# A convolution feed-forward on one core: seven products of quarters on every other weight step

## What is computed

```python
def conv_gated_ffn(h, w_up, conv_w, conv_b, w_down):
    u = h @ w_up                                   # 512 x 1024 times 1024 x 5632
    up = jnp.pad(u, ((0, 0), (1, 1), (0, 0)))
    u = up[:, :-2] * conv_w[0] + up[:, 1:-1] * conv_w[1] + up[:, 2:] * conv_w[2] + conv_b
    gate, val = u[..., :D_FF], u[..., D_FF:]
    return (jax.nn.silu(gate) * val) @ w_down      # D_FF = 2816
```

## Time and profile before

| | us |
|---|---|
| time, median of 3 runs (lowest, highest) | 3782.29 (3782.15, 3783.75) |
| the profiled execution, its own time | 3782.21 |
| its span, first to last instruction | 3780.4 |
| PE busy | 3712.6 (98%) |
| PEld busy | 3116.3 (82%) |
| DVE busy | 2598.0 (69%) |
| ACT busy | 1591.2 (42%) |
| POOL busy | 53.9 (1%) |
| granted TensorE clock, mean | 0.995 |

### The profile page before, as it was taken

How to read it: one execution, slowest core, us unless ns; L and a number is a source line. 1 busy time by engine, 2 the same in 40 slices (tenths; PEclk the granted TensorE clock), 3 DMA queues, 4 the chain that set the end, 5 groups by cost and what they waited for, 6 DMA issues and landing times. The chain is left out here.

```text
span 3780.4 us, 52721 instructions
## 1 busy us (share of the span) xinstructions
PE 3712.6 (98%) x20462; PEld 3116.3 (82%) x20462; DVE 2598.0 (69%) x3639; ACT 1591.2 (42%) x2347; POOL 53.9 (1%) x52
## 2 busy tenths in 40 slices
PE   9999999999999999999999999999999999999998
PEld 7998864988998998786598899865888888888887
DVE  8875666668884886576676887576767753567753
ACT  5552431544552554242254455266344432344431
POOL 0000000000000000000000000040000000000000
PEclk9999999999999999999999999999999999999999
DMA  3223220012222322221001222311322222222222
GB/s 139 100 95 106 86 90 1 1 45 100 100 98 91 109 102 95 102 89 67 1 1 68 99 101 91 113 43 42 127 81 100 100 91 99 103 87 100 100 85 82
DMA packets 52741, 314.85 MB, mean 83 GB/s; under 512 B 6640, under 2 KB 7474, under 8 KB 24440
## 3 DMA queue, kind: packets, MB, share of 16 engines
q1 hardware_dynamic: 52600, 312.94, 23.5%
HBM read 308.66 MB, written 2.10 MB: 82 GB/s over the span
## 5 line engine op out<-in xcount | busy, mean ns | idle before, releaser
L145 PE MATMUL bank<-hidden_hi,w_hi 128*128 128x512 f32 (+1 forms) x2112 | 764.9, 362 | 6.4 <-PEq L87 6.1
L146 PE MATMUL bank<-hidden_lo,w_hi 128*128 128x512 f32 (+1 forms) x2112 | 761.5, 361 | 0.0
L147 PE MATMUL bank<-hidden_hi,w_lo 128*128 128x512 f32 (+1 forms) x2112 | 761.4, 361 | 0.0
L285 DVE TENSOR_TENSOR w_lo<-w_raw,w_hi 128x2048 fp32r<-128x2048 f32 (+1 forms) x202 | 398.7, 1974 | 266.7 <-ACT w_hi L280 265.7
L280 ACT ACTIVATE w_hi<-w_raw 128x2048 fp32r<-128x2048 f32 (+1 forms) x202 | 334.9, 1658 | 565.8 <-PE bank L147 529.2
L145 PEld LDWEIGHTS bank<-hidden_hi,w_hi 128*128 128x128 f32 x2112 | 399.2, 189 | 79.4 <-issue 17.4
L147 PEld LDWEIGHTS bank<-hidden_hi,w_lo 128*128 128x128 f32 x2112 | 399.3, 189 | 60.8
L146 PEld LDWEIGHTS bank<-hidden_lo,w_hi 128*128 128x128 f32 x2112 | 399.3, 189 | 59.9 <-issue 0.2
L145 PE MATMUL bank<-ffn_act_hi,w_hi 128*128 128x512 f32 x704 | 273.9, 389 | 0.0
L146 PE MATMUL bank<-ffn_act_lo,w_hi 128*128 128x512 f32 x704 | 273.9, 389 | 0.0
L147 PE MATMUL bank<-ffn_act_hi,w_lo 128*128 128x512 f32 x704 | 273.9, 389 | 0.0
(11 more groups left out here) (536 smaller groups left out, 8014.8 us busy)
## 6 DMA issues: line engine op xcount, KB each, us to landing
w_raw<-in_w_gu SPq DMA_DIRECT2D x131, 1024.0 KB, 4.7
w_raw<-in_w_down SPq DMA_DIRECT2D x96, 704.0 KB, 4.0
w_raw<-in_w_in SPq DMA_DIRECT2D x28, 1024.0 KB, 4.7
w_raw<-in_w_xattn SPq DMA_DIRECT2D x24, 1024.0 KB, 4.8
w_raw<-in_w_out SPq DMA_DIRECT2D x8, 1024.0 KB, 5.8
w_raw<-in_w_xattn_o SPq DMA_DIRECT2D x8, 1024.0 KB, 4.8
hyena_dft<-in_c_dft SPq DMA_DIRECT2D x6, 1024.0 KB, 6.9
w_raw<-in_w_qkv SPq DMA_DIRECT2D x6, 1024.0 KB, 4.8
```

The lines of the kernel that those rows point to most:

```text
L145: nc.tensor.matmul(out, w_hi, x_hi, start=start, stop=False, skip_group_check=on)
L146: nc.tensor.matmul(out, w_hi, x_lo, start=False, stop=False, skip_group_check=on)
L147: return nc.tensor.matmul(out, w_lo, x_hi, start=False, stop=stop, skip_group_check=on)
L285: nc.vector.tensor_tensor(self.lo[:, slot, 0:width], self.raw[:, slot, 0:width], self.hi[:, slot, 0:width].bitcast(F32), ALU.subtract)\
```

## The change

`CONV_PLAIN = 6`: the first six steps of `conv_ffn` (three turns) stay plain. From the seventh step on slot 0 multiplies seven pairs of quarters, slot 1 stays plain: eight turns, each a seven step and a plain step. The four sums of input quarters are made and split by DVE and ACT during the first six steps (twelve short instructions of 256 columns and some of 1,024; they lie in the memory of the split activations, which are therefore made only at the end: `a_raw` keeps the activations until then). The gain columns of the layer's own norm come in as an argument for that. In a turn ACT also copies three partial sums and product 2 out of the banks (`keep`), and rounds the quarters and their sums; DVE makes the sums of weight quarters (`make_t13`, `make_t2`, `make_t4`), their rests (`lo_front`, `lo_t13`, `lo_r3`, `lo_t24`) and the results. `taps`, `gated`, `scaled_plain` are the old per-step work cut in functions.

```diff
+CONV_PLAIN = 6
...
+            def seven(r):
+                done, copied = S.sem("products"), S.sem("copied")
+
+                def part(at):
+                    return m.w_hi[:, 0, at], m.w_lo[:, 0, at]
+
+                pe.wait_ge(S.sem("front_split"), r + 1)
+                pe.wait_ge(S.sem("banks_free0"), r + begun + 1)
+                product(bank_a, *part(r0), quarter_of(0, first)).then_inc(done, 1)
+                product(bank_c, *part(t1), summed(0)).then_inc(done, 1)
+                pe.wait_ge(S.sem("w_split0"), r + begun + 1)
+                pe.wait_ge(copied, 4 * r + 1)
+                product(bank_a, t24_hi[:, 0, :], t24_lo[:, 0, :], summed(1), start=False).then_inc(done, 1)
+                product(bank_b, *part(r1), quarter_of(kh, first)).then_inc(done, 1)
+                pe.wait_ge(copied, 4 * r + 3)
+                product(bank_a, *part(t3), summed(2), start=False).then_inc(done, 1)
+                product(bank_c, r3_hi, r3_lo, summed(3), start=False).then_inc(done, 1)
+                pe.wait_ge(copied, 4 * r + 4)
+                product(bank_a, t24_hi[:, 1, :], t24_lo[:, 1, :], quarter_of(kh, later), start=False)\
+                    .then_inc(S.sem("w_used0"), 1)
+
             pair_pe(pe, nc, m, S, ring, 0, 0, h_tile, first="pairs", free="banks_free")
...
-            with pe.Fori(0, turns - 1) as i:
-                pair_pe(pe, nc, m, S, ring, i, 1, h_tile, free="banks_free")
-            for slot in range(2):
-                pe.wait_ge(S.sem(f"act_ready{slot}"), turns)
-            with pe.Fori(0, KD // 2) as i:
+            for i in range(1, begun):
+                pair_pe(pe, nc, m, S, ring, i, 0, h_tile, free="banks_free")
+            pe.wait_ge(S.sem("sums_split"), 4)
+            with pe.Fori(0, turns - begun) as r:
+                seven(r)
+                pair_pe(pe, nc, m, S, ring, r, begun, h_tile, free="banks_free", slots=(1,))
+
+            def down(d, b, i, split=False):
+                pe.wait_ge(S.sem(f"down_free{b}"), i + 1)
+                for slot in range(2):
+                    pe.wait_ge(S.sem(f"w_split{slot}"), d + turns + 1)
+                    for k in range(half):
+                        f = slot * half + k
+                        if split:
+                            pe.wait_ge(S.sem("act_split"), f + 1)
+                        w_hi, w_lo = ring.tile(slot, k)
+                        last = product3(nc, m.bank[4 + b][:, :], w_hi, w_lo, a_hi[:, f, :], a_lo[:, f, :],
+                                        start=(f == 0), stop=(f == NF - 1))
+                    last.then_inc(S.sem(f"w_used{slot}"), 1)
+
+            down(0, 0, 0, split=True)
+            down(1, 1, 0)
+            with pe.Fori(0, KD // 2 - 1) as i:
                 for b in range(2):
...
+            def beside_seven(r, i, width):
+
+                mid_tap(1, i, 0)
+                keep(P1, bank_a, 6 * r + 1)
+                mid_tap(1, i, 1)
+                keep(M5, bank_c, 6 * r + 2)
+                split_next(1, i + 1, width)
+                keep(U2, bank_a, 6 * r + 3)
+                silu(1, i)
+                keep(U3, bank_a, 6 * r + 5)
+
+            def beside_plain(i, after=None):
+
+                if after is not None:
+                    hi_front(after)
+                mid_tap(0, i, 0)
+                if after is not None:
+                    hi_t13(after)
+                mid_tap(0, i, 1)
+                if after is not None:
+                    hi_r3()
+                silu(0, i)
+                if after is not None:
+                    hi_t24(after)
+
...
+            with act.Fori(0, turns - begun - 1) as r:
+                beside_seven(r, r + begun - 1, UNIT)
+                beside_plain(r + begun, r + 1)
+            beside_seven(turns - begun - 1, turns - 2, UNIT)
+            split_next(0, turns, half_width)
+            mid_tap(0, turns - 1, 0)
+            mid_tap(0, turns - 1, 1)
+            silu(0, turns - 1)
+            for f in range(9):
+                act_hi(f)
+            plain(1, turns - 1, last=True)
+            split_next(1, turns, half_width)
+            for f in range(9, NF):
+                act_hi(f)
...
-            def turn(i, next_width, split_first=False):
...
-                    if not split_first or slot:
-                        ring.split_dve(dve, nc, S, slot, i + 1, next_width)
-                    dve.wait_ge(S.sem(f"act_hi{slot}"), i + 1)
-                    nc.vector.tensor_tensor(a_lo[:, a, :], gate_s[:, 0, :], a_hi[:, a, :].bitcast(F32),
-                                            ALU.subtract).then_inc(S.sem(f"act_ready{slot}"), 1)
...
+            def first_results(r):
+                dve.wait_ge(S.sem("copied"), 4 * r + 1)
+                dve.wait_ge(S.sem("products"), 6 * r + 4)
+                nc.vector.tensor_tensor(gate[:, first], moved[:, P1, :], bank_b, ALU.add).then_inc(S.sem("first_gate"), 1)
+                dve.wait_ge(S.sem("copied"), 4 * r + 4)
+                nc.vector.tensor_tensor(up[:, later], moved[:, M5, :], moved[:, U3, :], ALU.subtract)
+                dve.wait_ge(S.sem("first_gate"), r + 1)
+                nc.vector.tensor_tensor(gate[:, first], gate[:, first], m.rb[:, first], ALU.mult)
+
+            def later_results(r):
+                dve.wait_ge(S.sem("w_used0"), r + begun + 1)
+                nc.vector.tensor_tensor(up[:, first], bank_c, moved[:, U2, :], ALU.subtract).then_inc(S.sem("up_made"), 1)
+                nc.vector.tensor_tensor(gate[:, later], bank_a, m.rb[:, later], ALU.mult).then_inc(S.sem("scaled00"), 1)
+                dve.wait_ge(S.sem("scaled00"), r + begun + 1)
+                dve.sem_inc(S.sem("banks_free0"), 1)
+                dve.wait_ge(S.sem("up_made"), r + 1)
+                nc.vector.tensor_tensor(up, up, m.rb[:, :], ALU.mult).then_inc(S.sem("scaled01"), 1)
+
...
+            def beside_seven(r, i, width):
+
+                scaled_plain(1, i)
+                taps(1, i, 0)
+                taps(1, i, 1)
+                ring.split_dve(dve, nc, S, 1, i + 1, width)
+                gated(1, i)
+                first_results(r)
+
+            def beside_plain(i, after, results):
+
+                results()
+                make_t13(after)
+                make_t2(after)
+                taps(0, i, 0)
+                lo_front(after)
+                make_t4(after)
+                lo_t13(after)
+                taps(0, i, 1)
+                lo_r3(after)
+                lo_t24(after)
+                gated(0, i)
+
+            def act_rest(f):
+                dve.wait_ge(S.sem("act_hi"), f + 1)
+                nc.vector.tensor_tensor(a_lo[:, f, :], a_raw[:, f, :], a_hi[:, f, :].bitcast(F32), ALU.subtract)\
+                    .then_inc(S.sem("act_split"), 1)
+
...
+            beside_plain(begun - 1, 0, lambda: scaled_plain(0, begun - 1))
+            with dve.Fori(0, turns - begun - 1) as r:
+                with steps.loop(r, turns - begun - 1, 4):
+                    beside_seven(r, r + begun - 1, UNIT)
+                    beside_plain(r + begun, r + 1, lambda: later_results(r))
+            last = turns - begun - 1
+            beside_seven(last, turns - 2, UNIT)
+            later_results(last)
+            ring.split_dve(dve, nc, S, 0, turns, half_width)
+            taps(0, turns - 1, 0)
+            taps(0, turns - 1, 1)
+            gated(0, turns - 1)
+            for f in range(9):
+                act_rest(f)
+            scaled_plain(1, turns - 1)
+            taps(1, turns - 1, 0)
+            taps(1, turns - 1, 1)
+            ring.split_dve(dve, nc, S, 1, turns, half_width)
+            gated(1, turns - 1)
+            for f in range(9, NF):
+                act_rest(f)
```

More of the change, by code:

```diff
@@ L909, in conv_ffn @@
     turns = NF // 2
+    begun = CONV_PLAIN // 2
+    th, kh, quarter = T // 2, KD // 2, KD // 2 * P
+    first, later = slice(0, th), slice(th, T)
+    P1, M5, U2, U3 = range(4)
     with Stage(nc, name) as S:
         ring = Ring(S, m, early)
+        at = (nc.sbuf_base + 31) // 32 * 32
+        assert at % GRID == 0
         a_hi = S.sb("act_hi", [P, NF, T], F32R)
@@ new lines, in quarter_of, with summed, product @@
+            def quarter_of(k0, tokens):
+                return lambda k: (m.h_hi[:, k0 + k, tokens], m.h_lo[:, k0 + k, tokens])
+            def summed(n):
+                return lambda k: (sum_hi[:, n, k, :], sum_lo[:, n, k, :])
+            def product(out, w_hi, w_lo, x, start=True):
+                for k in range(kh):
+                    c = slice(k * P, (k + 1) * P)
+                    last = product3(nc, out, w_hi[:, c], w_lo[:, c], *x(k), start=start and k == 0,
+                                    stop=(k == kh - 1), on=not start)
+                return last
@@ new lines, in act_hi, with plain @@
+            def act_hi(f):
+                act.wait_ge(S.sem(f"act_raw{f % 2}"), f // 2 + 1)
+                nc.scalar.activation(a_hi[:, f, :], a_raw[:, f, :], ACT.Copy).then_inc(S.sem("act_hi"), 1)
```

(32 more changed lines are left out.)

214 lines of the change are left out of this document (143 added, 71 removed).

## The result

The changed kernel takes 3803.76 us (median of 5 runs, 3800.43 to 3804.29), the kernel before 3783.12 (5 runs, 3782.15 to 3783.75): ratio 1.0054, interval 1.0043 to 1.0066. It is slower, 20.6 us by the medians; the forecast was 3796.6, and its range, 3783 to 3805, holds the time by 1.2 us at its upper end. The profiled execution took 3803.96, its span 3802.1.

A forecast was written before the change was run, and what follows sets the result against it. TensorE bounded the old kernel; in the new loop DVE, ACT and TensorE would wait in a ring. A layer: 2.0 + 0 + 3.6 + 1.6 = 7.2, two layers 14.4, so 3782.2 + 14.4 = 3796.6 us; range 3783 to 3805.

The forecast's parts named there:

- The ring: In the new loop DVE, ACT and TensorE wait for one another; a pass takes 21.8 us, as before, saving nothing.
- DVE's stretch: DVE's work from a seven step's last matmul to the next plain evacuation, put at 12.0 us.
- the 0.23 behind the gating product: DVE's wait between the gating product and the plain evacuation, counted as 0.23 us of the 12.0.
- The second wait: TensorE waits 0.2 us before the fifth product of a seven step, for an ACT copy.
- DVE busy for 96% of a pass: In the new loop DVE works 96% of a pass and stands still only before the later results.
- The start: At the stage's start DVE reaches the loop late, so the first seven step ends 2.0 us a layer later (1 to 3).
- The stop before tile 10: At the first output TensorE stands still 3.6 us a layer, waiting for DVE's split of tile 10; bounds 2.5 to 5.
- The clock behind it: After the stop before tile 10 TensorE runs at the lower clock for eight matmuls, costing 1.6 us a layer.
- the term for the passes: Seven loop passes after the first add 0 us a layer (-5.5 to +3.5).
- the rival of 3802: Register waits make a pass 22.2, or the lower clock lasts eight microseconds: 2.5 to 3 us a layer more; chance 0.16.
- three signs of being wrong: Passes 21.0 to 21.3 apart, the stop before tile 10 under 2, or the first seven step ending where it did before.

The follow-up runs named there:

- copy first: Changed kernel with ACT copying product 1 out of its bank ahead of the first middle tap beside a seven step; 3795.3 us, ratio 1.0039.
- end reordered: Changed kernel with DVE's splits, weights and taps at the stage's end reordered and TensorE taking the second eleven tiles in two sweeps; 3803.4 us, ratio 1.0057.
- end swapped: Changed kernel, end in two sweeps with six second-output tiles between them, DVE splitting those weights before the last eleven activations; 3794.3 us, ratio 1.0031.
- eight plain steps first: Changed kernel with eight instead of six plain steps ahead of the first seven step (CONV_PLAIN = 8); 3795.3 us, ratio 1.0034.
- extra beside: Changed kernel plus one unread DVE instruction of 512 columns beside the seven step, before the gating product; 3801.6 us, ratio 1.0054.
- extra in the stretch: Changed kernel plus one unread DVE instruction of 512 columns between the seven step's end and the plain evacuation; 3810.2 us, ratio 1.0076.
- written out: Changed kernel with the seven turns of its loop as straight code on TensorE, ACT and DVE instead of a register loop; 3788.0 us, ratio 1.0016.
- three edits: Changed kernel with loop in straight code, eight plain steps first and the first reordered end together; 3785.5 us, ratio 1.0009.

## Why the prediction was right, and where not

- **The ring: right, its size 0.26 too small.** TensorE waits before the third product, released by ACT's copy, as said, 0.66 where I had 0.4 to 0.5; the two runs with the extra instruction and the one with the copy first show the ring. A pass is 22.06 and not 21.8. The rest of it is 9.77, as reckoned; DVE's stretch was 12.29 for 12.0, and the term that failed is the 0.23 behind the gating product, which at the end of a register loop is 0.50. The seven passes of a layer (six of 22.06, one of 21.51) cost 1.6, where I had 0.
- **The second wait: right.** Some 0.2 is lost before the fifth product in every pass, as foreseen, though the brackets show no idle time there; with the copy first it is an idle time of 0.55.
- **DVE busy for 96% of a pass: wrong,** 87%; its hand-overs inside the pass are idle time, not work, and it stands still before the evacuation (0.51) and the first tap (0.77) too, not only before the later results (0.38).
- **The start: 1.6 a layer for 2.0** (the first seven step ends 72.6 behind the stage's start in end reordered and end swapped, in the layer where the clock holds, and 71.0 before). But behind its 2.1 stop the clock fell as well, in both layers of this profile (73.9), and that took 1.3 a layer more that the sum did not have. (The change has sixteen sum instructions of 256 columns in all, not twelve; the twelve of this term are those behind step 3.)
- **The stop before tile 10: 3.56 for 3.6,** released by DVE, in both layers.
- **The clock behind it: 1.6 foreseen, 1.7 in layer 1 and 2.8 in layer 2** (8 and 12 matmuls of 0.43 instead of 0.226, and the first one behind the stop at 0.34 and 0.59). The rule of the Trainium skill cited there (TensorE: Matmul & The Clock Gate, HAM oscillation) is borne out by these rows.
- **Sum.** 7.2 a layer was forecast; it is 1.6 + 1.3 + 1.6 + 3.6 + 1.7 = 9.8, and 10.8 in layer 2. What failed is the term for the passes, set to 0, and the clock, reckoned for one stop of the two. The range holds the time with 1.2 us to spare, which is partly luck: 14.4 us were forecast and 20.6 came. The time lies nearest to the rival of 3802, and by both of that rival's reasons, longer passes and a longer low clock. None of the three signs of being wrong came.

## What to carry to other kernels

When a faster engine stage hands over to others twice per pass, add up the ring that these hand-overs close, start to start, with the loop's own costs read from a loop of the same engines; an engine that is busy for 87% can be part of the ring that sets the pass. When work is moved to a stage's end, count the whole backlog of the engine that does it: here a change of its order alone only moved the wait, and what hid the backlog was to give the waiting engine work that needs none of it. A stop of a matmul engine can have a second price, the lower clock behind it: here 1.3 to 2.8, behind every stop of 3.6 and most of those of 2.1.

## What the runs showed of the hardware

- The same instructions in straight code instead of a register loop: gating to evacuation 0.03 idle for 0.50 (0.40 with eight plain steps first; 0.21 behind the loop's last turn), a tap pair 0.78 for 0.90 (start to start), ACT's tap 0.73 behind the evacuation for 0.97. The stretch fell from 12.29 to 11.61 and the rest from 9.77 to 9.52, together 0.93 a pass.
- A stop of 2.1 at the first seven step was followed by a lower granted clock in 7 of 10 cases (two layers each of the changed kernel, copy first, extra beside, end reordered, end swapped; in copy first it stands before the fifth product), which cost 1.3 to 1.4 us. A stop of 2.7 there (extra in the stretch) was followed by one in 1 of 2 layers, a stop of 1.8 (written out) in neither; a stop of 2.1 before the second output (end reordered, three edits) in 3 of 4. Behind all 14 stops of 3.6 or more before tile 10 it fell, for 1.6 to 2.8; behind those of 1.5 and less at the second output the loss was 0.1. What decides between the two outcomes at 2.1 stays open.
